# Sums of squares of the norms sent chunk by chunk behind the producer's groups, and the scaling of a norm sent at the head of a pipeline step

## The chip, the cores and the metric

The kernel runs on the 8 cores of one Trainium2 chip, one prompt sequence of 2048 tokens and 16 of the 128 sample tokens on each; the cores exchange nothing. The metric is the device time of the slowest core in microseconds (us), over several runs. TensorE multiplies matrices into PSUM (8 banks of 512 f32 columns per partition), VectorE and ScalarE work elementwise, POOL and SP issue transfers. Each engine works through its own list in order and waits for the others by semaphores.

## The reference

```python
for i in range(4):                       # d_model 1024, d_ff 2816
    sh1, sc1, g1, sh2, sc2, g2 = split(silu(c) @ w_ada[i] + b_ada[i])
    h = rmsnorm(x, norm_mix[i]) * (1 + sc1) + sh1
    out = pool_mixer(h) if i % 2 == 0 else gmlp_mixer(h)
    x = x + g1 * out                     # out ends in a 1024 x 1024 projection
    h = rmsnorm(x, norm_ffn[i]) * (1 + sc2) + sh2
    x = x + g2 * ((silu(h @ w_gate[i]) * (h @ w_up[i])) @ w_down[i])
y = rmsnorm(x, norm_final)
# rmsnorm(x, g) = x * rsqrt(mean(x*x, axis=-1) + 1e-6) * g
# pool_mixer: causal window means (2, 4, 8, 16) minus h, per group 256 x 256, scale, @ w_out
# gmlp_mixer: u, v = split(h @ w_in); v = layernorm(v); causal 128 x 128 mix of v per chunk; (u * v) @ w_out
```

The nine RMS norms (two in each layer and the final one) are what the change is about.

## The kernel before

x is kept transposed on chip as `xT`: 8 chunks of 128 channels on the partitions, tokens along the free axis, in f32. Tokens are worked on in five blocks in the order SB (the 16 sample tokens), then blocks 0 to 3 of 512 prompt tokens. Weights come in tiles of 512 KB into a ring of eight slots (`wsl`), issued on POOL's queue.

A norm has two parts. `norm_a(key, b)` takes a PSUM bank, and for each of the 8 chunks ScalarE squares `xT` into one of three buffers `sq` and TensorE multiplies it with `ones_m` (all 1/1024), so that the bank ends up with the mean of squares on all partitions. The bank is held until `norm_b`: ScalarE computes Ln and Exp(-0.5) into `rstd`, then for each chunk VectorE forms `tmp` = xT * A * rstd and ScalarE writes `hT` = tmp + shift in bf16. For SB the chunks are three tiny VectorE operations and one ScalarE copy (`hs` to `hT`).

The stages of a layer run in a software pipeline: `pipeline(stages, order)` calls in step s stage 0 for the s-th block, stage 1 for the block before it, and so on. The list of calls is the list of each engine's instructions. A pooling layer has seven stages: the producer of x (the load of x, or the last down projection of the layer before), norm_a and norm_b of the first norm, `zpool` (group matmul, a copy of its result `arena` by ScalarE and VectorE, a matmul with window matrices `pmat`, a copy into `wk`), the out projection, norm_a and norm_b of the second norm. A gMLP layer has a pipeline of producer, norm_a, norm_b and `v_stage` (the v half of w_in, layernorm statistics by VectorE, `vA` and `vB`), then `v_flush` and `u_phase`, then a pipeline of out projection, norm_a and norm_b. The final norm is pipelined behind the last down projection, with `final_b` doing its scaling, transposes and output.

A producer works on a block in eight groups oc = 0 to 7: 8 matmuls of 512 columns (6 in the last down projection, whose group of rows has three tiles) into one bank, and then `x_update`, in which VectorE adds the gated bank to chunk oc of `xT`. After the second norm follows gate/up of the FFN, whose first ScalarE operation is a Silu on the gate bank (`sq<-ps`). Every matmul is recorded by `mm` (line 346), every transpose by `tr` (349), every ScalarE activation by `ACT` (357) and every VectorE product of this kind by `STT` (376), so rows are told apart by their tiles.

Of the kernel before, what the change touches and what calls it, by code (L numbers as in the profile page):

```python
# [169 lines left out]
def build_program(cfg):  # L170
# [105 lines left out]
    bONES = P.buf("ones")  # L276
# [37 lines left out]
    def nxt(key, n):  # L314
        v = state[key]
        state[key] = (v + 1) % n
        return v
# [44 lines left out]
    def VCOPY(out, in_, r, w):  # L362
        P.op("vector", lambda e: e.tensor_copy(out=out, in_=in_), r=r, w=w)
# [28 lines left out]
        ACT(out, in_, AF.Ln, r=list(r) + [bONES], w=w, bias=epsc[0:npart, :], scale=1.0)  # L392
        ACT(out, out, AF.Exp, r=w, w=w, scale=-0.5)

    def pipeline(stages, order, per_step=None):
        n = len(order)
        for step in range(n + len(stages) - 1):
            if per_step is not None:
                per_step()
            for k, stg_ in enumerate(stages):  # L400
                jj = step - k
                if 0 <= jj < n:
                    stg_(order[jj])

    ORDER = [SB] + list(range(NPB))

# [82 lines left out]
    bstg = [bR0, [bR1]]  # L489
    xl = {"n": 0}  # L490

    def xload_block(b):
        if b == SB:
            q = xl["n"] % 2
            xl["n"] += 1
            DMA("sync", stg[q][0:NS, :], xs[:, :], "xin%d" % q, w=bstg[q])
            bk = alloc_bank()
            for c in range(8):
                tr(ps[:, bk, c * 16:(c + 1) * 16], stg[q][0:NS, c * 128:(c + 1) * 128], ident[0:NS, 0:NS],
                   r=bstg[q] + [bCST], w=[PSB[bk]])  # L500
            VCOPY(xT[:, :, SEQ:SEQ + NS], ps[:, bk, 0:128].rearrange("p (c n) -> p c n", c=8),
                  r=[PSB[bk]], w=[X[c][SB] for c in range(8)])
            return
        for tt in range(4 * b, 4 * b + 4):
            q = xl["n"] % 2
            xl["n"] += 1
            DMA("sync", stg[q], xp[tt * 128:(tt + 1) * 128, :], "xin%d" % q, w=bstg[q])
            bk = alloc_bank(2)
            for c in range(8):
                tr(ps[:, bk + c // 4, (c % 4) * 128:(c % 4 + 1) * 128], stg[q][:, c * 128:(c + 1) * 128],  # L510
                   ident, r=bstg[q] + [bCST], w=[PSB[bk + c // 4]])
            for hh in range(2):
                o_ap = xT[:, 4 * hh:4 * hh + 4, tt * 128:(tt + 1) * 128]
                i_ap = ps[:, bk + hh, :].rearrange("p (c n) -> p c n", c=4)
                wb = [X[c][b] for c in range(4 * hh, 4 * hh + 4)]
                if hh == 0:
                    ACOPY(o_ap, i_ap, r=[PSB[bk + hh]], w=wb)
                else:
                    VCOPY(o_ap, i_ap, r=[PSB[bk + hh]], w=wb)

    nst = {}

    def norm_a(key, b):
        col0, n = blocks[b]
        bk = alloc_bank()
        for c in range(8):
            q = nxt("sq", 3)
            ACT(sq[:, q, 0:n], xT[:, c, col0:col0 + n], AF.Square, r=[X[c][b]], w=[SQ[q]])
            mm(ps[:, bk, 0:n], ones_m[:, :], sq[:, q, 0:n], c == 0, c == 7, r=[SQ[q], bONES], w=[PSB[bk]])
        nst[(key, b)] = bk  # L530
        held_banks.add(bk)

    def norm_rstd(key, b):
        col0, n = blocks[b]
# [46 lines left out]
    def make_outproj(i, W2d, src, SRC, m):  # L581
        par = i % 2
        st_ = {"tiles": None, "done": 0}

        def stage(b):
            if st_["tiles"] is None:
                ada_need(i, m)
                st_["tiles"] = [wget_cols(W2d, t * 256) for t in range(4)]
            col0, n = blocks[b]
            for oc in range(8):  # L590
                s, wv = st_["tiles"][oc // 2]
                oc2 = oc % 2
                bk = alloc_bank()
                for k in range(8):
                    mm(ps[:, bk, 0:n], wv[:, k, oc2 * 128:(oc2 + 1) * 128], src(k, col0, n), k == 0, k == 7,
                       r=[SLOT[s], SRC[k][b]], w=[PSB[bk]])
                x_update(bk, oc, b, par, m)
            st_["done"] += 1
            if st_["done"] == NB:
                for s, _ in st_["tiles"]:  # L600
                    wrel(s)
        return stage
# [266 lines left out]
    def make_ffn(i):  # L869
        par = i % 2  # L870
        groups = [[0, 1, 2, 3], [4, 5, 6, 7], [8, 9, 10]]

        def gate_up(grp):
            for ti, t in enumerate(grp):
                sg, gvw = wget_cols(ffn_w_gate[i], t * 256)
                su, uvw = wget_cols(ffn_w_up[i], t * 256)
                for fc in range(2):
                    wc = 2 * ti + fc
                    for b in ORDER:
                        col0, n = blocks[b]  # L880
                        bg = alloc_bank()
                        for k in range(8):
                            mm(ps[:, bg, 0:n], gvw[:, k, fc * 128:(fc + 1) * 128], hT[:, k, 16 + col0:16 + col0 + n],
                               k == 0, k == 7, r=[SLOT[sg], H[k][b]], w=[PSB[bg]])
                        bu = alloc_bank()
                        for k in range(8):
                            mm(ps[:, bu, 0:n], uvw[:, k, fc * 128:(fc + 1) * 128], hT[:, k, 16 + col0:16 + col0 + n],
                               k == 0, k == 7, r=[SLOT[su], H[k][b]], w=[PSB[bu]])
                        q = nxt("sq", 3)
                        ACT(sq[:, q, 0:n], ps[:, bg, 0:n], AF.Silu, r=[PSB[bg]], w=[SQ[q]])  # L890
                        TT(wk[:, wc, col0:col0 + n], ps[:, bu, 0:n], sq[:, q, 0:n], ALU.mult,
                           r=[PSB[bu], SQ[q]], w=[WK[wc][b]])
                wrel(sg)
                wrel(su)
                if ada_allow(i + 1):
                    ada_pop(2)

        def make_down(grp):
            st_ = {"sd": None, "done": 0}
            nk = 2 * len(grp)  # L900

            def stage(b):
                if st_["sd"] is None:
                    ada_need(i, 5)
                    st_["sd"] = [wget_rows(ffn_w_down[i], t * 256) for t in grp]
                col0, n = blocks[b]
                for oc in range(8):
                    bk = alloc_bank()
                    for kk in range(nk):
                        s, dv = st_["sd"][kk // 2]  # L910
                        mm(ps[:, bk, 0:n], dv[:, kk % 2, oc * 128:(oc + 1) * 128], wk[:, kk, col0:col0 + n],
                           kk == 0, kk == nk - 1, r=[SLOT[s], WK[kk][b]], w=[PSB[bk]])
                    x_update(bk, oc, b, par, 5)
                st_["done"] += 1
                if st_["done"] == NB:
                    for s, _ in st_["sd"]:
                        wrel(s)
            return stage

        def front():  # L920
            for gi, grp in enumerate(groups):
                gate_up(grp)
                if gi < len(groups) - 1:
                    dn = make_down(grp)
                    for b in ORDER:
                        dn(b)
                    if ada_allow(i + 1):
                        ada_pop(1)
            return make_down(groups[-1])
        return front  # L930
# [35 lines left out]
    prev_stage = xload_block  # L966
    for i in range(DEPTH):
        pool_layer = (i % 2 == 0)
        n1a = (lambda b, i=i: norm_a((i, 0), b))
        n1b = (lambda b, i=i, pl=pool_layer: norm_b(i, 0, pl, b))  # L970
        n2a = (lambda b, i=i: norm_a((i, 1), b))
        n2b = (lambda b, i=i, pl=pool_layer: norm_b(i, 1, pl, b))

        def step_pop(i=i):
            if ada_allow(i):
                ada_pop(2)

        if pool_layer:
            zpool, outp = make_pool(i)
            pipeline([prev_stage, n1a, n1b, zpool, outp, n2a, n2b], ORDER, per_step=step_pop)  # L980
        else:
            gmlp_prep(i)
            v_stage, v_flush, u_phase, outp = make_gmlp(i)
            pipeline([prev_stage, n1a, n1b, v_stage], ORDER, per_step=step_pop)
            v_flush()
            u_phase()
            pipeline([outp, n2a, n2b], ORDER, per_step=step_pop)
        ada_need(i, 5)
        if i == 0:
            for j in range(NPOOL):  # L990
                DMA("sync", nps[j, :, 0:PB - 1, :], sp[j, :, 1:PB, :], "out_hist")
        prev_stage = make_ffn(i)()
    pipeline([prev_stage, (lambda b: norm_a("fin", b)), final_b], ORDER)

    finals = ["out_hist", "out_np", "out_ns", "out_v", "out_y0", "out_y1"]
    stats = P.emit(nc, st, finals)
# [77 lines left out]
```

How the kernel before makes its waits and increments, by code:

```python
                def body(engine, e=e):  # L122
                    waited = {}
                    nwait = 0
                    for i, o in enumerate(self.ops[e]):
                        for t in o.deps:
                            if t[0] == "e":
                                name = "E_" + t[1]
                                val = cum[t[1]][t[2]]
                            else:
                                name = "D_" + t[1]
                                val = t[2] if t[2] is not None else self.dmacnt[t[1]]
                            if waited.get(name, 0) < val:
                                engine.wait_ge(sems[name], val)
                                waited[name] = val
                                nwait += 1
                        ins = o.fn(engine)
                        if o.dma is not None:
                            ins.then_inc(sems["D_" + o.dma], 16)
                        elif sig[e][i]:
                            ins.then_inc(sems["E_" + e], 1)
                    if e == "sync":
                        for sname in final_waits:
                            if sname in self.dmacnt:
                                engine.wait_ge(sems["D_" + sname], self.dmacnt[sname])
                    stats[e] = (len(self.ops[e]), nwait)
```

## Time and profile before

| | |
|---|---|
| median of 3 runs | 3476.02 us (3443.03 to 3523.37) |
| profiled execution, its own time | 3086.7 us |
| its span on the slowest core | 3084.9 us (all cores 3074.6 to 3084.9) |
| mean granted TensorE clock | 0.935 on that core, 0.935 to 0.940 on all |
| TensorE busy | 2735.5 us, 89% |
| VectorE busy | 1258.8 us, 41% |
| ScalarE busy | 732.7 us, 24% |
| POOL busy | 226.6 us, 7% |
| read from HBM, written | 291.39 MB, 10.67 MB |

The span is from the first to the last instruction of one core in one execution. A granted clock of 1.00 is TensorE's full 2.4 GHz, 0.50 is 1.2 GHz. Busy time of TensorE includes matmuls at the lower clock. All rows below are of core 5, the slowest.

### The profile page before, as it was taken

To read this page: it belongs to the slowest core of one execution; us is meant where nothing else is said; L and a number is where in the kernel's file an instruction comes from. 1 tells how busy PE (TensorE), PEld (TensorE's weight loads), DVE (VectorE), ACT (ScalarE), POOL (GpSimd) and SP (SyncE) were. 2 spreads that over 40 slices of the span, in tenths; PEclk is the share of its full clock that TensorE was granted. 3 is DMA by queue.
4 is the path that set the end of the run, shared out by engine and by line. 5 is a ranking of instruction groups with operands and counts; after the bars stand their busy time and mean duration, and the time that the engine had idled before them with its cause. 6 is when DMAs were issued, how large, how long until landed. Compare 5 with 4: busy or idle time off the path is not lost.

```text
span 3084.9 us, 47999 instructions; the slowest of 8 cores (3074.6 to 3084.9 us)
## 1 busy us (share of the span) xinstructions
PE 2735.5 (89%) x16951; PEld 1381.3 (45%) x16951; DVE 1258.8 (41%) x2764; ACT 732.7 (24%) x1396; POOL 226.6 (7%) x273
## 2 busy tenths in 40 slices
PE   1568899999878989999977799999987979999997
PEld 1344344444464434444434344444455434444443
DVE  1356323242675533324266623233367451323246
ACT  0343410101450241010144510111163061010122
POOL 2000010110001001101100010101000000000000
PEclk9579899999988989999988899999998989999996
DMA  9725362635304325343520343544312222132202
GB/s 154 127 54 87 40 83 35 83 41 77 49 1 63 40 36 83 45 72 50 73 35 1 49 57 53 73 72 62 56 21 29 28 28 42 14 55 28 35 2 110
DMA packets 247873, 165.57 MB, mean 54 GB/s; under 512 B 5267, under 2 KB 230987, under 8 KB 247610
## 3 DMA queue, kind: packets, MB, share of 16 engines
q0 software_dynamic: 238928, 137.77, 34.2%
q1 hardware_dynamic: 8714, 24.72, 2.4%
q8 instruction: 144, 2.36, 0.3%
q14 instruction: 87, 0.71, 0.1%
HBM read 291.39 MB, written 10.67 MB: 98 GB/s over the span
## 4 chain that ended last, share of the span: by engine, by line
PE 80%; ACT 6%; DVE 5%; issue 4%; DMA 4%; DVEq 0%; ACTq 0%; POOL 0%; SPq 0%; POOLq 0%
PE ps L346 77%; ACT hT L357 2%; PE ps L349 2%; DMA wsl<-w_ada 2%; ACT sq L357 2%; DMA arena<-xp 2%; DVE tmp L376 1%; ACT rstd L357 1%; DVE wk L376 1%; DVE small L763 1%; ACT arena L357 0%; DVE small L761 0%; ACT small L357 0%; DVEq L134 0%; DVE Amod L372 0%
## 5 line engine op out<-in xcount | busy, mean ns | idle before, releaser
L346 PE MATMUL ps<-hT,wsl 128*128 128x512 bf16 (+1 forms) x7680 | 1384.5, 339 | 20.5 <-ACT sq L357 20.5
L346 PEld LDWEIGHTS ps<-hT,wsl 128*128 128x128 bf16 x7680 | 639.9, 98 | 748.6 <-issue 39.5
L346 PE MATMUL ps<-wk,wsl 128*128 128x512 bf16 (+1 forms) x4800 | 878.6, 341 | 13.0 <-DVE t16b L366 9.1
L366 DVE TENSOR_TENSOR wk<-ps,sq 128x512 bf16<-128x512 f32 (+1 forms) x440 | 253.3, 587 | 960.9 <-PE ps L346 949.5
L346 PEld LDWEIGHTS ps<-wk,wsl 128*128 128x128 bf16 x4800 | 404.7, 98 | 471.9 <-issue 34.8
L357 ACT ACTIVATE sq<-ps 128x512 bf16<-128x512 f32 (+1 forms) x440 | 225.1, 515 | 1486.0 <-PE ps L346 1483.5
L376 DVE SCALAR_TENSOR_TENSOR xT<-ps,mod,xT 128x512 f32<-128x512 f32 x512 | 377.8, 749 | 377.0 <-PE ps L346 376.5
L357 ACT ACTIVATE sq<-xT 128x512 bf16<-128x512 f32 (+1 forms) x360 | 170.1, 536 | 469.6 <-PE ps L346 304.6
L376 DVE SCALAR_TENSOR_TENSOR tmp<-xT,Amod,rstd 128x512 f32<-128x512 f32 x256 | 173.1, 746 | 104.0 <-ACT rstd L357 103.7
L346 PE MATMUL ps<-wsl,hT 128*128 128x256 bf16 (+1 forms) x1344 | 186.1, 303 | 20.3 <-DVE wk L376 15.5
L346 PE MATMUL ps<-sq,ones_m 128*128 128x512 bf16 (+1 forms) x360 | 121.7, 384 | 72.5 <-ACT sq L357 55.8
L357 ACT ACTIVATE hT<-tmp,mod 128x512 bf16<-128x512 f32 x256 | 172.0, 721 | 32.7 <-DVE tmp L376 32.2
L346 PEld LDWEIGHTS ps<-wsl,hT 128*128 128x128 bf16 (+1 forms) x1344 | 141.5, 108 | 52.4 <-issue 23.8
L331 POOL DMA_DIRECT2D wsl<-w_ada x96 | 84.6, 889 | 836.5 <-PE ps L346 835.4
L346 PEld LDWEIGHTS ps<-sq,ones_m 128*128 128x128 bf16 x360 | 34.9, 98 | 159.3 <-issue 145.8
L331 POOL DMA_DIRECT2D wsl<-ffn_w_gate x44 | 38.7, 879 | 908.1 <-PE ps L346 908.1
L349 PE MATMUL ps<-cstt,arena 128*128 128x128 f32 (+2 forms) x179 | 35.4, 365 | 75.7 <-DMA arena<-xp 43.0
L346 PE MATMUL ps<-scT,wsl 128*128 128x17 bf16 x1536 | 48.5, 172 | 39.6 <-DMA wsl<-w_ada 36.9
L366 DVE TENSOR_TENSOR wk<-ps,wk 128x512 bf16<-128x512 f32 (+1 forms) x80 | 46.0, 586 | 65.8 <-PE ps L346 65.6
L346 PE MATMUL ps<-pmat_sb,arena 128*128 128x128 bf16 x496 | 32.2, 221 | 42.8 <-ACT arena L360 38.2
L346 PEld LDWEIGHTS ps<-scT,wsl 128*128 128x128 bf16 x1536 | 47.0, 97 | 50.8 <-issue 40.9
L376 DVE SCALAR_TENSOR_TENSOR wk<-ps,colv,arena 128x128 bf16<-128x128 f32 x256 | 68.4, 341 | 0.0
(74 smaller groups left out, 855.0 us busy)
## 6 DMA issues: line engine op xcount, KB each, us to landing
wsl<-w_ada POOLq DMA_DIRECT2D x96, 512.0 KB, 11.8
wsl<-ffn_w_gate POOLq DMA_DIRECT2D x44, 512.0 KB, 7.3
wsl<-ffn_w_up POOLq DMA_DIRECT2D x44, 512.0 KB, 8.9
wsl<-ffn_w_down POOLq DMA_DIRECT2D x44, 512.0 KB, 7.5
arena<-xp SPq DMA_DIRECT2D x16, 512.0 KB, 8.4
wsl<-gmlp_w_in POOLq DMA_DIRECT2D x16, 512.0 KB, 9.1
yp<-arena SPq DMA_DIRECT2D x16, 512.0 KB, 2.6
wsl<-pool_w_out POOLq DMA_DIRECT2D x8, 512.0 KB, 9.2
```

The source lines that it names most:

```text
L331: P.op("gpsimd", lambda e: e.dma_start(out=dst, in_=src), w=[SLOT[s]], dma="w%d" % s)
L346: P.op("tensor", lambda e: e.matmul(out, lhsT, rhs, start=start, stop=stop), r=r, w=w)
L349: P.op("tensor", lambda e: e.transpose(out, in_, idn), r=r, w=w)
L357: P.op("scalar", lambda e: e.activation(out=out, in_=in_, func=func, **kw), r=r, w=w)
L366: P.op("vector", lambda e: e.tensor_tensor(out=out, in0=in0, in1=in1, op=op), r=r, w=w)
L376: P.op("vector", lambda e: e.scalar_tensor_tensor(out=out, in0=in0, scalar=scalar, in1=in1, op0=op0, op1=op1), r=r, w=w)
L763: P.op("vector", lambda e: e.bn_stats(out=small[0:npart, o + 6:o + 12], in_=ps[0:npart, bk + 1, :]), r=[PSB[bk + 1]], w=[bsm])
```

## The change

`pipeline` now takes items with explicit offsets, in the order in which they are called in a step. An item of four parts is a producer with its offset and a norm_a with its own: the producer gets a callback `co` and calls it after each of its groups, and `co(c)` does chunk c of norm_a for the block before. `norm_a` now does one chunk; at c = 0 it takes the bank. Where the producer has no block left, the eight chunks are called in a row. `xload_block` calls `co` twice for each 128 tokens; the out projection and the down projection once for each oc (the edits of the two are alike, one is shown). And the norm_b items stand first in every list, so they are called ahead of the producer in a step; `final_b` too. The amount of work is the same on every engine.

```diff
--- before.py
+++ after.py
@@ -392,15 +392,29 @@
         ACT(out, in_, AF.Ln, r=list(r) + [bONES], w=w, bias=epsc[0:npart, :], scale=1.0)
         ACT(out, out, AF.Exp, r=w, w=w, scale=-0.5)
 
-    def pipeline(stages, order, per_step=None):
+    def pipeline(items, order, per_step=None):
         n = len(order)
-        for step in range(n + len(stages) - 1):
+        max_off = max(max(it[1], it[3] if len(it) > 2 else 0) for it in items)
+        for step in range(n + max_off):
             if per_step is not None:
                 per_step()
-            for k, stg_ in enumerate(stages):
-                jj = step - k
-                if 0 <= jj < n:
-                    stg_(order[jj])
+            for it in items:
+                fn, off = it[0], it[1]
+                jj = step - off
+                has_fn = 0 <= jj < n
+                if len(it) > 2:
+                    co_fn, co_off = it[2], it[3]
+                    jc = step - co_off
+                    has_co = 0 <= jc < n
+                    if has_fn and has_co:
+                        fn(order[jj], (lambda c, bb=order[jc]: co_fn(bb, c)))
+                    elif has_fn:
+                        fn(order[jj], None)
+                    elif has_co:
+                        for c in range(8):
+                            co_fn(order[jc], c)
+                elif has_fn:
+                    fn(order[jj])
 
     ORDER = [SB] + list(range(NPB))
 
...
@@ -517,18 +534,22 @@
                     ACOPY(o_ap, i_ap, r=[PSB[bk + hh]], w=wb)
                 else:
                     VCOPY(o_ap, i_ap, r=[PSB[bk + hh]], w=wb)
+            if co is not None:
+                co(2 * ti)
+                co(2 * ti + 1)
 
     nst = {}
 
-    def norm_a(key, b):
+    def norm_a(key, b, c):
         col0, n = blocks[b]
-        bk = alloc_bank()
-        for c in range(8):
-            q = nxt("sq", 3)
-            ACT(sq[:, q, 0:n], xT[:, c, col0:col0 + n], AF.Square, r=[X[c][b]], w=[SQ[q]])
-            mm(ps[:, bk, 0:n], ones_m[:, :], sq[:, q, 0:n], c == 0, c == 7, r=[SQ[q], bONES], w=[PSB[bk]])
-        nst[(key, b)] = bk
-        held_banks.add(bk)
+        if c == 0:
+            bk = alloc_bank()
+            nst[(key, b)] = bk
+            held_banks.add(bk)
+        bk = nst[(key, b)]
+        q = nxt("sq", 3)
+        ACT(sq[:, q, 0:n], xT[:, c, col0:col0 + n], AF.Square, r=[X[c][b]], w=[SQ[q]])
+        mm(ps[:, bk, 0:n], ones_m[:, :], sq[:, q, 0:n], c == 0, c == 7, r=[SQ[q], bONES], w=[PSB[bk]])
 
     def norm_rstd(key, b):
         col0, n = blocks[b]
...
@@ -595,6 +616,8 @@
                     mm(ps[:, bk, 0:n], wv[:, k, oc2 * 128:(oc2 + 1) * 128], src(k, col0, n), k == 0, k == 7,
                        r=[SLOT[s], SRC[k][b]], w=[PSB[bk]])
                 x_update(bk, oc, b, par, m)
+                if co is not None:
+                    co(oc)
             st_["done"] += 1
             if st_["done"] == NB:
                 for s, _ in st_["tiles"]:
...
@@ -966,9 +991,9 @@
     prev_stage = xload_block
     for i in range(DEPTH):
         pool_layer = (i % 2 == 0)
-        n1a = (lambda b, i=i: norm_a((i, 0), b))
+        n1a = (lambda b, c, i=i: norm_a((i, 0), b, c))
         n1b = (lambda b, i=i, pl=pool_layer: norm_b(i, 0, pl, b))
-        n2a = (lambda b, i=i: norm_a((i, 1), b))
+        n2a = (lambda b, c, i=i: norm_a((i, 1), b, c))
         n2b = (lambda b, i=i, pl=pool_layer: norm_b(i, 1, pl, b))
 
         def step_pop(i=i):
@@ -977,20 +1002,21 @@
 
         if pool_layer:
             zpool, outp = make_pool(i)
-            pipeline([prev_stage, n1a, n1b, zpool, outp, n2a, n2b], ORDER, per_step=step_pop)
+            pipeline([(n1b, 2), (n2b, 6), (prev_stage, 0, n1a, 1), (zpool, 3), (outp, 4, n2a, 5)],
+                     ORDER, per_step=step_pop)
         else:
             gmlp_prep(i)
             v_stage, v_flush, u_phase, outp = make_gmlp(i)
-            pipeline([prev_stage, n1a, n1b, v_stage], ORDER, per_step=step_pop)
+            pipeline([(n1b, 2), (prev_stage, 0, n1a, 1), (v_stage, 3)], ORDER, per_step=step_pop)
             v_flush()
             u_phase()
-            pipeline([outp, n2a, n2b], ORDER, per_step=step_pop)
+            pipeline([(n2b, 2), (outp, 0, n2a, 1)], ORDER, per_step=step_pop)
         ada_need(i, 5)
         if i == 0:
             for j in range(NPOOL):
                 DMA("sync", nps[j, :, 0:PB - 1, :], sp[j, :, 1:PB, :], "out_hist")
         prev_stage = make_ffn(i)()
-    pipeline([prev_stage, (lambda b: norm_a("fin", b)), final_b], ORDER)
+    pipeline([(final_b, 2), (prev_stage, 0, (lambda b, c: norm_a("fin", b, c)), 1)], ORDER)
 
     finals = ["out_hist", "out_np", "out_ns", "out_v", "out_y0", "out_y1"]
     stats = P.emit(nc, st, finals)
```

TensorE's list in the second pipeline of layer 1 (`wk,wsl` is the out projection, `sq,ones_m` a norm matmul, `hT,wsl` the gate/up that follows). Before:

```order
417 L346 MATMUL ps<-wk,wsl 128x512 x64
418 L346 MATMUL ps<-sq,ones_m 128x16 x8
419 L346 MATMUL ps<-wk,wsl 128x512 x64
420 L346 MATMUL ps<-sq,ones_m 128x512 x8
421 L346 MATMUL ps<-wk,wsl 128x512 x64
```

and now, from the second full block of the out projection on:

```order
569 L346 MATMUL ps<-wk,wsl 128x512 x8
570 L346 MATMUL ps<-sq,ones_m 128x512
571 L346 MATMUL ps<-wk,wsl 128x512 x8
572 L346 MATMUL ps<-sq,ones_m 128x512
573 L346 MATMUL ps<-wk,wsl 128x512 x8
```

The eight norm matmuls of a block stood behind its successor's 64; now one stands behind each group of 8, and TensorE comes to the first of them after 8 matmuls.

ScalarE's list at the same place (`sq<-xT` are squares, `rstd` Ln and Exp, the CAST and `hT<-tmp,mod` the writes of norm_b, `sq<-ps` the Silu). Before:

```order
180 L357 ACTIVATE sq<-xT 128x16 x8
181 L357 ACTIVATE sq<-xT 128x512 x8
182 L357 ACTIVATE rstd<-ps,epsc 128x16
183 L357 ACTIVATE rstd<-rstd 128x16
184 L360 CAST hT<-hs32 128x16 x8
185 L357 ACTIVATE sq<-xT 128x512 x8
186 L357 ACTIVATE rstd<-ps,epsc 128x512
187 L357 ACTIVATE rstd<-rstd 128x512
188 L357 ACTIVATE hT<-tmp,mod 128x512 x8
189 L357 ACTIVATE sq<-xT 128x512 x8
```

and now:

```order
204 L357 ACTIVATE sq<-xT 128x16 x8
205 L357 ACTIVATE rstd<-ps,epsc 128x16
206 L357 ACTIVATE rstd<-rstd 128x16
207 L360 CAST hT<-hs32 128x16 x8
208 L357 ACTIVATE sq<-xT 128x512 x8
209 L357 ACTIVATE rstd<-ps,epsc 128x512
210 L357 ACTIVATE rstd<-rstd 128x512
211 L357 ACTIVATE hT<-tmp,mod 128x512 x8
212 L357 ACTIVATE sq<-xT 128x512 x8
```

Before, two sets of squares stood ahead of the first Ln, so each Ln read a bank that had been filled a step earlier. Now each Ln stands directly behind the squares of its own block, and the next block's squares behind that block's norm_b.

## Rows read from the trace of the kernel before

**Rows 1.** The page, part 1: busy us, share of the span, instructions.
```profile
PE 2735.5 (89%) x16951; PEld 1381.3 (45%) x16951; DVE 1258.8 (41%) x2764; ACT 732.7 (24%) x1396; POOL 226.6 (7%) x273
```
**Rows 2.** The page, part 4: the chain that ended last, by engine.
```profile
PE 80%; ACT 6%; DVE 5%; issue 4%; DMA 4%; DVEq 0%; ACTq 0%; POOL 0%; SPq 0%; POOLq 0%
```
**Rows 3.** Waits of TensorE: us in total, times, longest us.
```profile
PE ps L346 <- ACT sq L357: 76.4, 49, 7.9
...
PE ps L346 <- ACT arena L360: 38.2, 7, 6.3
```
**Rows 4.** Timeline, TensorE, out projection of layer 1: start, us, what [idle before].
```profile
1060.15 0.81 PE L346 MATMUL ps<-sq,ones_m 128*128 128x512 bf16 x3
...
1063.69 13.97 PE L346 MATMUL ps<-wk,wsl 128*128 128x512 bf16 x64
...
1089.13 4.12 PE L346 MATMUL ps<-sq,ones_m 128*128 128x512 bf16 x8 [7.92 <-ACT sq L357]
1093.04 11.65 PE L346 MATMUL ps<-hT,wsl 128*128 128x16 bf16 x64
1109.50 10.78 PE L346 MATMUL ps<-hT,wsl 128*128 128x512 bf16 x50 [4.81 <-ACT sq L357]
```
**Rows 5.** Timeline, ScalarE, the same stretch.
```profile
1045.89 0.25 ACT L357 ACTIVATE rstd<-ps,epsc 128x16 f32<-128x16 f32 x1
...
1052.48 1.67 ACT L357 ACTIVATE sq<-xT 128x512 bf16<-128x512 f32 x3
1060.63 2.71 ACT L357 ACTIVATE sq<-xT 128x512 bf16<-128x512 f32 x5 [6.49 <-PE ps L346]
1063.24 0.67 ACT L357 ACTIVATE rstd<-ps,epsc 128x512 f32<-128x512 f32 x1
...
1070.88 1.65 ACT L357 ACTIVATE sq<-xT 128x512 bf16<-128x512 f32 x3
```
**Rows 6.** Timeline, VectorE, the same stretch.
```profile
1064.73 5.42 DVE L376 SCALAR_TENSOR_TENSOR tmp<-xT,Amod,rstd 128x512 f32<-128x512 f32 x8 [3.56 <-ACT rstd L357]
```
**Rows 7.** Timeline, TensorE, last down projection of layer 0.
```profile
795.09 0.22 PE L346 MATMUL ps<-sq,ones_m 128*128 128x16 bf16 x3
...
796.71 10.52 PE L346 MATMUL ps<-wk,wsl 128*128 128x512 bf16 x48
```
**Rows 8.** Timeline, ScalarE, last down projection of layer 1.
```profile
1568.43 1.28 ACT L357 ACT_TABLE_LOAD   x1
```
**Rows 9.** Timeline, TensorE, v stage of layer 1, behind a wait.
```profile
901.54 6.37 PE L346 MATMUL ps<-wsl,hT 128*128 128x256 bf16 x32 [6.14 <-DVE wk L376]
```
**Rows 10.** Windows, TensorE: window, us, busy (matmuls), granted clock, DMA share, GB/s.
```profile
360.00:380.00 20.00, 20.00 (x127) 1.00 0.87 106
...
901.00:907.00 6.00, 5.46 (x26) 0.50 0.00 1
...
1109.00:1116.00 7.00, 6.50 (x23) 0.55 0.00 0
```
**Rows 11.** Timeline, start of the v stage of layer 1: TensorE, and VectorE's third norm_b.
```profile
838.61 10.64 PE L346 MATMUL ps<-wsl,hT 128*128 128x256 bf16 x96
...
866.30 5.39 DVE L376 SCALAR_TENSOR_TENSOR tmp<-xT,Amod,rstd 128x512 f32<-128x512 f32 x8 [4.84 <-ACT rstd L357]
871.61 0.69 DVE L761 BATCH_NORM_STATS2 small<-ps 128x6 f32<-128x512 f32 x1
```
**Rows 12.** Timeline, TensorE, pooling pipeline of layer 2.
```profile
1596.00 0.57 PE L346 MATMUL ps<-pl,wsl 128*128 128x16 bf16 x16 [7.99 <-DVE pl L376]
1596.43 12.29 PE L346 MATMUL ps<-wk,wsl 128*128 128x512 bf16 x48
...
1619.96 1.01 PE L346 MATMUL ps<-pmat_sb,arena 128*128 128x128 bf16 x8 [5.59 <-ACT arena L360]
...
1669.70 1.21 PE L346 MATMUL ps<-pmat_sb,arena 128*128 128x128 bf16 x16 [6.17 <-ACT arena L360]
```
**Rows 13.** Timeline, TensorE, load of x in layer 0.
```profile
162.22 3.65 PE L349 MATMUL ps<-cstt,arena 128*128 128x128 f32 x16 [12.87 <-DMA arena<-xp]
```

More of the change, by code:

```diff
@@ L490, in build_program, with xload_block @@
     xl = {"n": 0}
-    def xload_block(b):
+    def xload_block(b, co=None):
         if b == SB:
@@ L502, in xload_block @@
                   r=[PSB[bk]], w=[X[c][SB] for c in range(8)])
+            if co is not None:
+                for c in range(8):
+                    co(c)
             return
-        for tt in range(4 * b, 4 * b + 4):
+        for ti, tt in enumerate(range(4 * b, 4 * b + 4)):
             q = xl["n"] % 2
@@ L583, in make_outproj, with stage @@
         st_ = {"tiles": None, "done": 0}
-        def stage(b):
+        def stage(b, co=None):
             if st_["tiles"] is None:
@@ L597, in stage @@
                 x_update(bk, oc, b, par, m)
+                if co is not None:
+                    co(oc)
             st_["done"] += 1
@@ L900, in make_down, with stage @@
             nk = 2 * len(grp)
-            def stage(b):
+            def stage(b, co=None):
                 if st_["sd"] is None:
@@ L913, in stage @@
                     x_update(bk, oc, b, par, 5)
+                    if co is not None:
+                        co(oc)
                 st_["done"] += 1
```

## The prediction

> **What bounds the kernel now.** I read the page first. TensorE is busy 89% of a span of 3084.9 us [rows 1], and the chain that ended last runs 80% through TensorE, 6% through ScalarE and 5% through VectorE [rows 2]. So the time is TensorE's stream plus the places where that stream stands still. The waits of TensorE name two such places: 76.4 us in 49 waits for a square (or Silu) on ScalarE, 38.2 us in 7 for ScalarE's copies in the pooling stage [rows 3]. The timeline shows the first: a dense 512-column matmul takes 13.97/64 = 0.22 us, but between two groups of 64 output matmuls the eight norm matmuls need from 1060.15 to 1063.69, 3.54 us, since they follow ScalarE's squares (2.71 us for five, 0.54 each) and not their own 0.22 us [rows 4, 5].
>
> The same rows show what is hidden today. After the squares of one block ScalarE does norm_b of the block before it: Ln at 1063.24, Exp, then eight Identity writes paced by VectorE's eight products of 5.42 us, then at 1070.88 the first square of the next block [rows 5, 6]. All of this lies beside TensorE's 13.97 us group that starts at 1063.69. Norm_b costs nothing there.
>
> **What the change does to this.** (a) The norm matmul of chunk c is sent behind the producer's group c, so a full block's eight should cost 8 x 0.22 = 1.7 us. (b) norm_b is sent at the head of a step, directly behind the last norm matmul of the same block. Both engines' order lists show it. TensorE now meets its first norm matmul after only 8 (or 6) matmuls; ScalarE serves that matmul's square only after norm_b. (b) is what I think decides.
>
> Step 1, squares no longer waited for. Full block: 3.54 - 1.7 = 1.8 us. Nine norms have three such blocks each (the last block has no producer left beside it); I take three of layer 0 out, which lie under the loads of x. 24 x 1.8 = 43 us. Sample block: 795.09 to 796.71 is 1.6 us, of which 0.6 remains (0.22 for three) [rows 7]: 9 x 1.0 = 9 us. Together -52.
>
> Step 2, the new wait. From Ln to the end of the first square is 1070.88 + 0.55 - 1063.24 = 8.2 us, with 0.1 for the signal from TensorE 8.3 us [rows 5]. Against it TensorE has one group of eight, 1.7 us, or in the down projections of six, 10.52/8 = 1.3 us [rows 4, 7]. So it stands still for 6.6 or 7.0 us. VectorE's x update of that group is queued behind norm_b's products as well, and nobody needs it sooner. How often: each out projection of a gMLP layer twice (4), each of a pooling layer once (2), each down projection that feeds a norm of layer 1 or 3 twice (4), layer 2 twice (2, the second 6.0, as its Ln and Exp run beside zpool of the sample block). 6 x 6.6 + 4 x 7.0 + 13.0 = 81 us. The sample block's norm_b is small but serial: 1052.48 + 0.6 - 1045.89 = 7.2 us [rows 5], so 5.6 us in two out projections, and 6.0 in three down projections, where also a table load of 1.28 us comes onto the path [rows 8]: 33 us. Together 17 waits, +114.
>
> Step 3, the clock behind each wait. After the 6.14 us wait at 901.54 the granted clock is 0.50, the 1.2 GHz level, from 901 to 907 [rows 9, 10], and 32 matmuls take 6.37 us where 96 of their kind take 10.64 at full clock [rows 11]: 2.8 us lost. After the 4.81 us wait at 1109.50 it is 0.55 to 1116, 7 x 0.45 = 3.2 us. After the 7.99 us wait at 1596.00 the 48 matmuls behind it take 12.29 us instead of 10.52, 1.8 lost [rows 12, 7]. Dense work shows 1.00, the 2.4 GHz level [rows 10]. I take 2.7: 17 x 2.7 = +46. The Trainium skill (TensorE: Matmul & The Clock Gate, Part 1: The HAM clock gate) says of the ramp that for modeling its penalty is under 1% of a typical span. By that sentence this step would be at most 31 us and the sum 77; the three restarts above decide, since their prices are measured here.
>
> Step 4, the ends of the out projections. Before, two norm_b stand between the last squares and the first Silu, and TensorE, having started gate/up at 1093.04, stands 4.81 us at 1109.50 and loses 3.2 more to the clock [rows 4, 10]. Now one norm_b (7.7 + 1.28 us) stands there, less than the 11.7 us that TensorE has. The uncovered wait of 7.92 us stays. 4 x (-8.0 + 0.4) = -30.
>
> Step 5, the v stage of gMLP, which VectorE bounds from 871.61 on. Before, its first bn_stats after the third norm_b comes 33.0 us after 838.61, where the stage starts [rows 11]. Now that norm_b is ready early, but the squares of the last block come behind it, and only then the next v matmuls: four tiles at 3.55 on TensorE and 4.4 to ScalarE's last write 18.6, norm_b 7.7, squares 4.2 and 0.3, one v tile at half clock 5.3: 36.0. 2 x 3.0 = +6.
>
> Step 6, the pooling layers. zpool of the sample block finds VectorE free of norm_b: the 7.99 us wait shrinks by 5.3, the one of layer 0 by 3. zpool of the first full block loses its 5.59 us wait, but the next norm_b and eight squares then stand alone before TensorE: net +1.5 per layer. From there two norm_b stand ahead of ScalarE's copy for zpool: the 6.17 us wait grows by the sample block's 5.4, the wait of the block behind by 1.4 [rows 12]. -8.3 + 2 x 8.3 = +8.3.
>
> Step 7, the rest. In layer 0 the load of x waits 12.87 us for a transfer [rows 13] and hides norm_b; -2, bounded by -14 (three uncovered norm_a of 4.2 us vanish) and +8 (one wait of step 2 shows). In the last pipeline TensorE's own transposes cover the end of final_b, so no wait of step 2 arises; a table load comes onto the path once: +2.
>
> Sum: -52 + 114 + 46 - 30 + 6 + 8.3 - 2 + 2 = **+92 us**. Against the profiled execution's own 3086.7 us that is 3179 us, +3.0%. The three runs shown have a median of 3476.02, 389 us above it. If those 389 us lie in TensorE's 2735.5 us, its matmuls are 14% longer there: step 1 gives 7 less, the waits are 0.25 us shorter each (-4), and the loss of half clock against the slower one is 0.4 us smaller each (-7). +88 us, **3564 us**, +2.5%.
>
> **Rivals.**
> - *The wait comes, its price is smaller.* The 17 restarts cost little, because full clock comes back within a few matmuls: without step 3 the sum is 92 - 46 = +46 us, 3522 us, within 2%. For it: after the 7.99 us wait at 1596.00 the loss was only 1.8 us [rows 12]. Against it: the 6 us at 0.50 [rows 10]. Chance 0.24.
> - *Faster.* norm_b ends within TensorE's first group, so the wait of step 2 never shows and steps 1 and 4 stand: 92 - 114 - 46 = -68 us, 3408 us, 2% faster. The place is the first norm matmul behind each producer's first group; the point from which it decides is a chain from Ln to first square under 1.7 us. The rows have 8.2, and all its pieces are in ScalarE's queue in that order. It would need norm_b's start to move ahead, which the last norm matmul forbids. Chance 0.06.
> - *Worse in the pooling layers.* The head of a step has norm_b twice there (blocks s-2 and s-6). If the x updates held back behind them on VectorE also keep PSUM banks from TensorE, each of the six such steps costs another norm_b of 7.7 us: +46, 3610 us. Against it: at most two banks stay held at once now. Chance 0.10.
> - *The change does nothing.* Excluded by the order lists; the squares do sit between the groups.
>
> **How the numbers follow.** The likeliest case keeps 0.60 and its own range is +60 to +120 us; the term with the widest bounds is step 7 with step 3. What a measurement can tell from no change is about 2%, 69.5 us. Of the likeliest case about four fifths lie above that (0.50), with the pooling case 0.60; I add 0.04 for the part of the first rival that keeps half the clock loss: slower 0.64. Within: 0.30. Faster: 0.06. The range goes from +46 us less the 33 us that the lowest run lies under the median, 3489, to the pooling case and 30 of the 47 us that the highest lies above it, 3640.
>
> **What would show it.** In the profile after: the norm matmuls no longer in eights, and the wait of TensorE for a square up from 76 us to about 150 or more, in pieces of 6 to 7 us, one for each step, always at the first norm matmul of a step (step 2); granted clock 0.50 behind each (step 3), so a mean clock under 0.935; the gap between two output groups gone elsewhere, 0.2 us for each chunk (step 1); no wait of 4.8 us in gate/up after an out projection (step 4); the ScalarE copy waits in the pooling stage fewer but longer (step 6). I am wrong if ScalarE takes its first square of a step within 2 us of the producer's start, or if TensorE restarts at 1.00.

## The result

The changed kernel is slower: 1.0225 times the time of the kernel before, 95% interval 1.0211 to 1.0239, over ten runs of each, in turns on the same chips; that is about 70 us on 3087 us. In some executions of either kernel (six of the ten of before, all three of the runs shown at first among them, and two of the change's ten) the cores of one die run at a lower granted clock and need up to 3523 us, so the ratio leaves these out, and the two medians, 3157.6 us now and 3327.66 us before, can't be set against each other.

The profiled execution took 3157.93 us with a span of 3156.4 us, 71.5 us above that of before. In the page TensorE's busy time fell by 18 us; what grew is the time in which it stands still [rows 1].

```profile
PE 2717.2 (86%) x16951; PEld 1372.1 (43%) x16951; DVE 1262.9 (40%) x2764; ACT 745.8 (24%) x1396; POOL 226.6 (7%) x273
```

The waits of TensorE (us in total, times, longest) say on what: squares on ScalarE from 76.4 to 194.6 us, and for `rstd` from 2.7 to 34.0, while the copies of the pooling stage fell from 38.2 us in 7 waits to 20.9 in 4 [rows 3]. First the row for `rstd` before, then the three rows now:

```profile
PE ps L346 <- ACT rstd L357: 2.7, 4, 1.2
```
```profile
PE ps L346 <- ACT sq L357: 194.6, 38, 12.4
...
PE ps L346 <- ACT rstd L357: 34.0, 20, 8.4
...
PE ps L346 <- ACT arena L360: 20.9, 4, 6.3
```

The timeline of TensorE in the out projection of layer 1 is the place of [rows 4]. Each line has the start, the length, the matmuls and, in brackets, the idle time before them and what ended it. One step, from one block's last norm matmul to the next block's:

```profile
1065.74 0.38 PE L346 MATMUL ps<-sq,ones_m 128*128 128x512 bf16 x1
1067.05 1.89 PE L346 MATMUL ps<-wk,wsl 128*128 128x512 bf16 x8 [0.93 <-ACT rstd L357]
1074.70 0.59 PE L346 MATMUL ps<-sq,ones_m 128*128 128x512 bf16 x1 [5.77 <-ACT sq L357]
1075.09 3.60 PE L346 MATMUL ps<-wk,wsl 128*128 128x512 bf16 x8
1078.50 0.40 PE L346 MATMUL ps<-sq,ones_m 128*128 128x512 bf16 x1
1078.74 1.89 PE L346 MATMUL ps<-wk,wsl 128*128 128x512 bf16 x8
...
1091.48 1.89 PE L346 MATMUL ps<-wk,wsl 128*128 128x512 bf16 x8 [0.93 <-ACT rstd L357]
```

From the second row to the last a step takes 24.43 us; before it took 17.35 (1046.34 to 1063.69, [rows 4]):

```profile
1046.34 13.97 PE L346 MATMUL ps<-wk,wsl 128*128 128x512 bf16 x64
```

Now the first group of eight waits 0.93 us for its bank and runs, then TensorE stands 5.77 us at the first norm matmul, and the next group takes 3.60 us, not 1.89. From the fifth row on the interleaving works as meant: 1.94 us a chunk, no wait. ScalarE over the same stretch shows what TensorE waits for:

```profile
1066.21 0.69 ACT L357 ACTIVATE rstd<-ps,epsc 128x512 f32<-128x512 f32 x1 [5.20 <-PE ps L346]
1066.99 0.63 ACT L357 ACTIVATE rstd<-rstd 128x512 f32<-128x512 f32 x1
1068.58 5.36 ACT L357 ACTIVATE hT<-tmp,mod 128x512 bf16<-128x512 f32 x8 [0.95 <-DVE tmp L376]
1073.84 2.18 ACT L357 ACTIVATE sq<-xT 128x512 bf16<-128x512 f32 x4
```

ScalarE was idle for 5.20 us before the Ln, because its bank was complete only with the last norm matmul, and from there the chain to the end of the first square is 1073.84 + 0.55 - 1066.21 = 8.2 us, as in [rows 5]. The windows (window, us, busy, granted clock) price the restart: 0.50 and 0.56 behind two of the waits, and 0.98 in gate/up behind the stage, where [rows 10] had 0.55 from 1109 on.

```profile
1050.00:1054.00 4.00, 4.00 (x11) 0.50 0.00 0
1075.00:1079.00 4.00, 4.00 (x12) 0.56 0.00 0
...
1129.00:1146.00 17.00, 17.00 (x93) 0.98 0.00 0
```

### The profile page after: what moved, and what is told of

Its sections match the earlier page's. It is cut to its first block, busy times and chain, and to the rows that moved or that the text cites. A ratio compares the mean times of both kernels' runs of the same rounds, so it can differ in the third digit from the quotient of the medians.

```text
span 3156.4 us, 47810 instructions; the slowest of 8 cores (3147.7 to 3156.4 us)
## 1 busy us (share of the span) xinstructions
PE 2717.2 (86%) x16951; PEld 1372.1 (43%) x16951; DVE 1262.9 (40%) x2764; ACT 745.8 (24%) x1396; POOL 226.6 (7%) x273
## 4 chain that ended last, share of the span: by engine, by line
PE 81%; ACT 6%; DVE 5%; DMA 3%; issue 3%; DVEq 0%; ACTq 0%; POOL 0%; SPq 0%; POOLq 0%
PE ps L346 79%; ACT hT L357 4%; DMA wsl<-w_ada 2%; PE ps L349 2%; DMA arena<-xp 1%; ACT rstd L357 1%; DVE tmp L376 1%; DVE wk L376 1%; ACT sq L357 1%; DVE tmp L366 1%; DVE small L786 0%; ACT small L357 0%; DVE small L784 0%; DVEq L134 0%; DVE hs L366 0%
## 5 line engine op out<-in xcount | busy, mean ns | idle before, releaser
L346 PE MATMUL ps<-wk,wsl 128*128 128x512 bf16 (+1 forms) x4800 | 936.0, 348 | 31.1 <-ACT rstd L357 16.8
L346 PE MATMUL ps<-sq,ones_m 128*128 128x512 bf16 (+1 forms) x360 | 138.9, 400 | 196.2 <-ACT sq L357 194.6
L357 ACT ACTIVATE sq<-xT 128x512 bf16<-128x512 f32 (+1 forms) x360 | 180.6, 541 | 364.4 <-PE ps L346 193.0
L346 PE MATMUL ps<-wsl,hT 128*128 128x256 bf16 (+1 forms) x1344 | 174.8, 291 | 30.5 <-DVE wk L376 15.1
L349 PE MATMUL ps<-cstt,arena 128*128 128x128 f32 (+2 forms) x179 | 33.9, 350 | 59.2 <-DMA arena<-xp 29.5
L370 DVE TENSOR_SCALAR mod<-ps,colv 128x17 f32<-128x17 f32 x192 | 44.2, 232 | 53.3 <-PE ps L346 38.4
## 6 DMA issues: line engine op xcount, KB each, us to landing
wsl<-w_ada POOLq DMA_DIRECT2D x96, 512.0 KB, 11.9
```

Source lines behind the costliest of these rows:

```text
L346: P.op("tensor", lambda e: e.matmul(out, lhsT, rhs, start=start, stop=stop), r=r, w=w)
L349: P.op("tensor", lambda e: e.transpose(out, in_, idn), r=r, w=w)
L357: P.op("scalar", lambda e: e.activation(out=out, in_=in_, func=func, **kw), r=r, w=w)
L370: P.op("vector", lambda e: e.tensor_scalar(out=out, in0=in0, scalar1=s1, scalar2=None, op0=op0), r=r, w=w)
```

## The experiments

E1 to E4 shared one chip and the runs of before (lowest 3081.80 us), E6 and E7 another (3082.64), and E8 a third (3081.90); there is no E5. Each row has the ratio to the runs of before on the same chip.

| run | ratio to before, 95% | profiled execution |
|---|---|---|
| the change | 1.0225 (1.0211 to 1.0239) | 3157.93 us |
| E1 interleaving only | 1.0070 (1.0052 to 1.0088) | 3105.25 us |
| E2 norm_b ahead only | 0.9934 (0.9915 to 0.9953) | 3062.85 us |
| E3 late squares | 0.9786 (0.9756 to 0.9816) | 3018.67 us |
| E4 filled waits | 1.0125 (1.0102 to 1.0148) | 3121.47 us |
| E6 half way | 1.0124 (1.0079 to 1.0169) | 3122.74 us |
| E7 bank only | 1.0235 (1.0188 to 1.0281) | 3169.8 us |
| E8 late squares, final_b behind | 0.9759 (0.9742 to 0.9777) | 3013.94 us |

The stages of the profiled executions, in us, from TensorE's first matmul of a stage to that of the next:

| stage | before | change | E1 | E2 | E3 | E4 |
|---|---|---|---|---|---|---|
| layer 0 to gate/up | 322.7 | 321.3 | 317.0 | 320.2 | 310.2 | 317.0 |
| layer 1, out projection | 81.1 | 101.0 | 89.1 | 81.8 | 75.7 | 95.1 |
| gate/up behind it, to the first down projection | 125.5 | 118.0 | 124.9 | 117.4 | 117.0 | 117.5 |
| layer 2 to gate/up | 213.2 | 233.5 | 213.9 | 213.8 | 202.8 | 227.9 |
| last down projection to the end | 129.1 | 127.0 | 119.7 | 133.1 | 126.9 | 125.5 |

**E1, interleaving only.**

```diff
-[(n1b, 2), (prev_stage, 0, n1a, 1), (v_stage, 3)]
+[(prev_stage, 0, n1a, 1), (n1b, 2), (v_stage, 3)]
-[(n2b, 2), (outp, 0, n2a, 1)]
+[(outp, 0, n2a, 1), (n2b, 2)]
 # the pooling and the last pipeline alike
```

> The norm matmuls stay between the producer's groups as in the change, norm_b goes back behind the producer, where it was before. My theory (the first square of a step stands behind norm_b in ScalarE's list, wherever in the step norm_b is called): VectorE now begins norm_b after the producer's last x update, so TensorE's wait at the first norm matmul of a step is 0.75 + 5.4 + 0.6 - 1.7 = about 5 us instead of 5.8, and the 4.8 us wait of gate/up with its clock loss comes back in four places: 3145 to 3175 us. Rival (the place of norm_b at the head of a step is what costs, the interleaving is a pure gain of 52 us): 3025 to 3045 us.

Measured: 3105 us, between the two; both numbers missed. The mechanism of my theory is in the trace: TensorE's wait at the first norm matmul of a step is still there, 5.86 us, without norm_b at the head of the step.

```profile
1067.51 1.89 PE L346 MATMUL ps<-wk,wsl 128*128 128x512 bf16 x8
1075.26 0.58 PE L346 MATMUL ps<-sq,ones_m 128*128 128x512 bf16 x1 [5.86 <-ACT sq L357]
```

ScalarE had Ln and Exp done at 1063.24 + 0.63 and then waited 5.20 us for VectorE's products, which stand behind the producer's last x update:

```profile
1063.24 0.63 ACT L357 ACTIVATE rstd<-rstd 128x512 f32<-128x512 f32 x1
1069.07 5.41 ACT L357 ACTIVATE hT<-tmp,mod 128x512 bf16<-128x512 f32 x8 [5.20 <-DVE tmp L376]
```

What my number left out is how often: with norm_b behind the producer, the squares that come behind the norm_b of block 1 have no producer beside them any more, so a pipeline has two such waits and not three (the out projection of layer 1 shows 5.63 and 5.86; the change has 5.19, 5.77 and 5.84, and 0.54, 0.93 and 0.93 before the first groups). A wait and its clock are 8 to 9 us, the larger part of the 11.9 us between the table's 89.1 and 101.0.

**E2, norm_b ahead only.**

```diff
+    def spread(co, oc, first):
+        if co is not None:
+            for c in range(8):
+                at = 7 if first == 8 else first + c * (8 - first) // 8
+                if at == oc:
+                    co(c)
...
                 x_update(bk, oc, b, par, m)
-                if co is not None:
-                    co(oc)
+                spread(co, oc, 8)
 # the down projection alike; xload_block calls all eight behind its last 128 tokens
```

> norm_b stays at the head of the step as in the change, but the eight norm matmuls of a block go in one piece behind the producer's last group, as before the change. My theory: norm_b hides beside the eight groups, no wait at a first norm matmul, the 3.5 us for eight norm matmuls stay as before, and the ends of the out projections keep their gain of 7.6 us each: 3087 - 30 and some us from the pooling stages, 3045 to 3070 us. Rival (norm_b at the head of a step is what costs): 3120 us or more.

Measured: 3063 us, ratio 0.9934, as my theory had it. The out projection of layer 1 takes 81.8 us as before, and gate/up behind it loses its 4.8 us wait and the clock (117.4 against 125.5). So norm_b at the head of a step is worth 0.7% by itself; only the last stage gets longer by it, 133.1 us against 129.1. TensorE in that stage reads like [rows 4], a group of 64 and then 3.5 us for eight norm matmuls:

```profile
1036.04 13.97 PE L346 MATMUL ps<-wk,wsl 128*128 128x512 bf16 x64
1049.85 0.81 PE L346 MATMUL ps<-sq,ones_m 128*128 128x512 bf16 x3
1051.10 2.45 PE L346 MATMUL ps<-sq,ones_m 128*128 128x512 bf16 x5 [0.44 <-ACT sq L357]
```

**E3, late squares.**

```diff
                 x_update(bk, oc, b, par, m)
-                if co is not None:
-                    co(oc)
+                spread(co, oc, 4)
 # spread as in E2; the down projection alike, with spread(co, oc, 5)
```

> As the change, but the producer calls for its norm chunks only from group 4 on, two for each group (in the last down projection from group 5 on: 3, 3, 2). Five groups of the out projection are 8.6 us, six of the down projection 7.8 us, against a chain of 8.3 us from Ln to the first square. My theory: 17 waits of 6 us and their half-clock stretches of 2 us each vanish from 3157 us, which gives 3015 to 3045 us, below both kernels. Rival (cutting TensorE's stream with norm matmuls is what costs): it stays above 3087 us.

Measured: 3018.67 us, ratio 0.9786: faster than both kernels, with the norm matmuls still between the producer's groups and the same norm_b at the head. Of the 105.1 us of waits for squares 82 stand before the blocks that have no producer beside them and 15 under the load of x; the eight that are left, 0.8 to 1.3 us each, are in the down projections, where six groups are 7.8 us and the chain 8.2. In the out projection of layer 1 TensorE is busy for 25.96 of 26 us at full clock:

```profile
PE ps L346 <- ACT sq L357: 105.1, 29, 12.4
```
```profile
1018.00:1044.00 26.00, 25.96 (x121) 1.00 0.02 2
```

ScalarE's chain is as long as ever, from 1020.96 to a first square at 1028.58, but TensorE now has 40 matmuls beside it:

```profile
1020.26 0.59 PE L346 MATMUL ps<-sq,ones_m 128*128 128x512 bf16 x2
1020.69 8.80 PE L346 MATMUL ps<-wk,wsl 128*128 128x512 bf16 x40
1029.44 0.79 PE L346 MATMUL ps<-sq,ones_m 128*128 128x512 bf16 x2
```

**E4, filled waits.**

```diff
                 x_update(bk, oc, b, par, m)
+                if co is not None and oc == 0 and (b == 3 or (b in (1, 2) and i % 2 == 1)):
+                    fb = alloc_bank()
+                    for _ in range(3):
+                        for k in range(8):
+                            mm(ps[:, fb, 0:n], wv[:, k, oc2 * 128:(oc2 + 1) * 128], src(k, col0, n), k == 0, k == 7,
+                               r=[SLOT[s], SRC[k][b]], w=[PSB[fb]])
 # the down projection alike, four times six
```

> As the change, but in the 17 places of step 2 (16 of them before a wait of 5 to 6.3 us) TensorE repeats the producer's first group three times (down projection: four times) into a bank that nobody reads, 24 matmuls, 5.2 us of extra work where it would stand still. It prices the clock alone. If the half clock behind each wait costs 2 us or more (step 3): 3157 - 34 to - 46, 3110 to 3125 us, with 24 extra matmuls in each place. If the restarts cost nothing (first rival): 3157 us, or some us more.

Measured: 3121.47 us, ratio 1.0125. With 408 matmuls more than the change the kernel is 36.5 us faster by the spans (3119.9 and 3156.4, not taken side by side) and 31 us by the ratios. The first 32 matmuls of a step now run through at 0.22 us each, 0.59 us of the wait are left, and the next group takes 1.89 where it took 3.60:

```profile
1052.04 7.07 PE L346 MATMUL ps<-wk,wsl 128*128 128x512 bf16 x32 [0.93 <-ACT rstd L357]
1059.70 0.38 PE L346 MATMUL ps<-sq,ones_m 128*128 128x512 bf16 x1 [0.59 <-ACT sq L357]
1059.92 1.89 PE L346 MATMUL ps<-wk,wsl 128*128 128x512 bf16 x8
```

Not all of the 36.5 us is the clock: 4.3 lie before the gate/up of layer 0, where one wait only was filled, and 1.5 in the last stage, where none was. From that gate/up to the last down projection are 2677.4 us in place of 2708.2, so 16 filled waits gave 30.8 us back. The clock behind a wait costs 1.9 us, some 33 us for the 17, and the wait itself is what remains.

**E6, half way.** As E3, with `spread(co, oc, 2)` in both producers.

> As the change, but the producer calls for its norm chunks from group 2 on (2, 1, 1, 2, 1, 1 for each group), so that TensorE has three groups before the first norm matmul of a step and not one. My theory, the chain of 8.3 us against what TensorE has: 3 x 1.73 = 5.2 us in the out projections leave a wait of 2.2 us (two to three bank-wait tenths included), 3 x 1.3 = 3.9 us in the down projections one of 3.5 us, against 5.8 and 6.3 us now. 17 places, about 3.2 us less each and some of the half clock: 3157 - 54 to - 80, 3077 to 3103 us. If the number of groups ahead did not matter, or only their being in one piece (the late squares took that away too), it would stay near 3157 or drop to 3017 us at once.

Measured: 3122.74 us, ratio 1.0124, outside what I had expected. But the span was 3088.0 to 3098.4 us on six cores and 3120 to 3121 us on the two others, at a granted clock of 0.927 and 0.928, and this makes it the least certain of the times; the six cores lie within the expectation. The waits of the two groups of cores agree (3.41 us on core 0 and on core 4). On core 0, out projection of layer 1:

```profile
1026.08 0.79 PE L346 MATMUL ps<-sq,ones_m 128*128 128x512 bf16 x2 [2.40 <-ACT sq L357]
...
1047.07 0.85 PE L346 MATMUL ps<-sq,ones_m 128*128 128x512 bf16 x2 [3.41 <-ACT sq L357]
```

The wait is 6.70 us with one group ahead, 3.41 with three, none with five: two groups more take off 3.3 us, which is their 3.5 us of work. I had expected 2.2 us because I had taken the 0.93 us of the bank off; it is part of the chain (E7).

**E7, bank only.**

```diff
         bk = nst.pop((key, b))
-        held_banks.discard(bk)
+        lazy.append([bk, 3])
 # alloc_bank counts these down and gives the bank back
```

> As the change, but the PSUM bank that norm_b gives back stays out of the next two allocations. In the change TensorE's first group of a step asks for just that bank and waits 0.93 us for the Ln that reads it. If the chain from the last norm matmul over Ln to the first square sets the end of the wait, the 0.93 us only move into the wait behind the first group, and the time stays at 3157 us within 5. If the bank wait is a cost of its own: 16 x 0.93 = 15 us less, 3142 us.

Measured: ratio 1.0235 against 1.0225, the same. The wait of 0.93 us at the head of the step is gone and stands in the next one, 6.85 where the change has 0.93 + 5.77:

```profile
1072.36 0.59 PE L353 MATMUL ps<-sq,ones_m 128*128 128x512 bf16 x1 [6.85 <-ACT sq L364]
```

**E8, late squares, final_b behind.** Against E3:

```diff
                     x_update(bk, oc, b, par, 5)
-                    spread(co, oc, 5)
+                    spread(co, oc, (5 if i < DEPTH - 1 else 0))
...
-    pipeline([(final_b, 2), (prev_stage, 0, (lambda b, c: norm_a("fin", b, c)), 1)], ORDER)
+    pipeline([(prev_stage, 0, (lambda b, c: norm_a("fin", b, c)), 1), (final_b, 2)], ORDER)
```

> The late squares, with one more edit: in the last pipeline final_b goes back behind the producer and the norm chunks are called from group 0 on, as in the run with interleaving only. The stage from the last down projection to the end took 119.7 us there and 126.9 us with the late squares, since final_b at the head of a step makes TensorE's transposes wait for the chain over Ln and Exp. My theory (each pipeline's part costs for itself): 3018 - 7 = 3011 us, within 4. Rival (the last stage gains nothing once the steps before it change): 3018 us.

Measured: median 3010.58 us, ratio 0.9759 (E3: 0.9786), about 8 us less than E3's 3018. It is the fastest version here, 2.4% under the kernel before. The two intervals overlap and the runs are not of one chip, but the traces show the place: the last down projection starts at nearly the same time, and from there to the end of the span are 121.8 us in E8 (span 3012.4) and 126.9 in E3. Two things are changed in that stage, the place of final_b and the group from which the chunks are called; which of them gives the 5 us is not shown. First E8, then E3:

```profile
2890.64 2.78 PE L346 MATMUL ps<-wk,wsl 128*128 128x16 bf16 x53
```
```profile
2890.24 9.26 PE L346 MATMUL ps<-wk,wsl 128*128 128x16 bf16 x84
```

## Why the prediction was right or wrong

The direction, the mechanism and its places were right; the time was not, since it was put on the wrong base.

- **The base: this step failed.** The prediction added its sum to the median of three runs, 3476.02 us, and took the 389 us by which that lies above the profiled execution for a part of every run ("If those 389 us lie in TensorE's 2735.5 us, its matmuls are 14% longer there"). They are not: the ten runs of before go from 3085.95 to 3523.37 us and those of the change from 3154.75 to 3504.98, eight of them under 3159. Against the profiled execution's 3086.7 us the same sum gave 3179 us and +3.0%; the measured ones are 3157.93 us and +2.25%. The range of 3489 to 3640 us holds neither the change's median of 3157.6 us nor more than one of its ten runs. A range that takes in the profiled execution's own time as a second base, or a forecast by that one alone, would have been sound.
- **Step 1**, 1.8 us for each covered block. A step of the change is 24.43 = 15.6 + 6.7 + 2.1 us, with 15.6 for 64 + 8 matmuls of 0.22 us, against 17.35. Right.
- **Step 2**, 17 waits, 114 us in all. Right. The rows of the change add up to 115 us: 21.9 in layer 1's down projection (1.82 + 5.79, 0.93 + 6.20, 0.93 + 6.27), 19.2 in its out projection, 26.3 in layer 2, 6.7 in layer 0, 21.8 and 19.2 in layer 3. I had not seen that 0.93 of each would be met at the first group, where TensorE asks for the bank that norm_b gives back; E7 shows that nothing hangs on it. A wait of the kind that I had put under the loads of layer 0 did appear there (5.78 us).
- **Step 3**, the clock, is the term that was mis-sized: 2.7 us each, 46 us; E4 measured 1.9 each, some 33 us. Two of the three rows I took it from had 6 to 7 us at about half clock behind the wait (0.50 and 0.55), and here it is mostly 3.4 to 4; the third, with 1.8 us lost, was near. The Trainium skill (TensorE: Matmul & The Clock Gate, Part 1: The HAM clock gate) has the penalty of the ramp under 1% of a typical span. From this the prediction estimated at most 31 us. E4's figures, 31 to 36.5 us, are 1.0 to 1.2% of the span for these 17 waits alone, at the limit of that sentence or over it; of the two figures, 31 and 46, the sentence's was the nearer.
- **Step 4**, 8.0 us for each end of an out projection: gate/up behind it took 8.0, 7.6, 7.1 and 6.9 us less in the four layers. Right.
- **Steps 5 and 6.** Layers 1 and 3 from the last down projection through the v stage: +23.6 and +21.9 us, where the prediction's terms give 26.0 (-6.4 of step 1, 21.3 of step 2, 8.1 of step 3, 3.0 of step 5); 2.4 of the difference are the clock. Layer 2 with its gate/up: +20.3 - 7.1 = +13.2, predicted 20.3. The two waits in which two norm_b stand ahead came out at 6.52 + 6.25 us in place of 6.17, where step 6 has 11.6. But the third wait of step 2 was 4.86 us, not 6.0, and 3.2 us is the clock; the rest, some 3 us, I did not take apart.
- **Step 7.** Layer 0 with its gate/up came out at -1.5 - 8.0 = -9.5 us where my steps had -2.4: the norm matmuls fit into TensorE's waits for transfers better than I gave them (those for `arena<-xp` fell from 43.0 to 29.5 us), towards the -14 end of its bound. The load's own waits differ by some us from run to run (the same code reached gate/up at 321.3 us in the change and 317.0 in E4, with one filled wait of 2 us in it). The last stage gave -2.2, predicted -4.4.
- Together: 92 predicted, 71.5 in the spans. 13 us of the gap are step 3 and 6 the rest of layer 0; what is left goes both ways and nearly cancels.
- **Rivals.** "The wait comes, its price is smaller" was the nearest of them, though the sum of +92 was nearer to 71.5 than its +46: the clock was worth some 33 us and not 0. "Faster" is refuted at its own point of decision: the chain is 8.2 us and not 1.7. "Worse in the pooling layers" did not happen: TensorE did wait for a bank there once in each layer (6.52 us in layer 2, 8.40 in layer 0, both for `rstd`), but layer 2 took less than the likeliest case gives it. This is also why the sign for step 6, copy waits "fewer but longer", came true by half: 4 in place of 7, but the longest still 6.3 us. That the change does both things that it says is shown by E1 and E2.

## What to carry to other kernels

Work that is cut up and strewn into a producer's stream must be ready when the stream reaches its first piece: count the producer's work ahead of that piece against the longest chain that stands before it in the other engine's list. Here 1.7 us stood against 8.3, and the same interleaving cost 2.3% or gained 2.1% depending on whether it began at group 0 or at group 4. Two edits that each look nearly neutral or good (E2 gains 0.7%, E1 costs 0.7%) can need the same engine at the same time, and together cost 2.3%: judge them together, and measure them apart.

## What the runs showed of the hardware that I had not expected

A stretch of idle TensorE costs more than its length, and useless matmuls can buy it back: 408 more matmuls made the kernel 36.5 us faster (E4), some 31 of them by the waits that they fill, since the granted clock behind a wait of about 6 us was 0.50 to 0.56 over 4 us, at or near 0.50, the 1.2 GHz level. Behind the waits of [rows 9, 10] it had been 6 to 7 us; why the stretches differ is open.
